# 26 of 88 gate and up pairs of a transformer kernel computed as a 2x2 block product of seven products

## The reference

```python
def swiglu(h, w_gate, w_up, w_down):
    return (jax.nn.silu(h @ w_gate) * (h @ w_up)) @ w_down

x = x + 0.5 * swiglu(rms_norm(x, norm_w[i, 0]), ffn_w_gate[i, 0], ffn_w_up[i, 0], ffn_w_down[i, 0])
```

## Time and profile before

| | us |
|---|---|
| median of 3 runs | 2694.77 |
| lowest and highest | 2693.09, 2696.92 |
| the profiled execution, first to last instruction | 2692.5 |
| TensorE busy in it | 2635.1 (98%) |
| VectorE, ScalarE, GpSimd busy | 1632.1, 869.7, 653.6 |

### The profile page before, as it was taken

The page is one execution under the profiler, slowest core; times in us unless marked ns, Lnnn a source line. Parts: engine busy times, 40 slices in busy tenths (PEclk is TensorE's granted clock), DMA queues, the critical chain, the costliest instruction groups (busy, mean ns, idle before and its releaser), DMA issues.

```text
span 2692.5 us, 32765 instructions
## 1 busy us (share of the span) xinstructions
PE 2635.1 (98%) x12738; PEld 2184.7 (81%) x12738; DVE 1632.1 (61%) x2391; ACT 869.7 (32%) x1501; POOL 653.6 (24%) x700
## 2 busy tenths in 40 slices
PE   8999999999999999999999999999999999899998
PEld 6888887778778888888888889988888878777886
DVE  5344468988846545565455657754343477768996
ACT  3101125666611101121001135621001035537995
POOL 2111221222322211221211247722211141012220
PEclk9999999999999999999999999999999999999999
DMA  4333333333324434445445330023333364037995
GB/s 124 98 94 101 95 94 107 96 105 102 94 81 138 141 111 147 133 118 148 125 128 146 104 106 2 9 71 101 94 98 98 92 82 64 15 125 281 373 368 228
DMA packets 457067, 325.80 MB, mean 121 GB/s; under 512 B 34657, under 2 KB 421042, under 8 KB 456658
## 3 DMA queue, kind: packets, MB, share of 16 engines
q1 hardware_dynamic: 435240, 287.22, 36.3%
q10 hardware_dynamic: 15050, 28.08, 3.4%
q0 software_dynamic: 6624, 8.41, 0.9%
HBM read 323.06 MB, written 16.32 MB: 126 GB/s over the span
## 4 chain that ended last, share of the span: by engine, by line
PE 91%; DVE 5%; ACT 2%; DMA 1%; issue 1%; SPq 0%; POOL 0%; DVEq 0%; ACTq 0%; POOLq 0%
PE bank L254 24%; PE bank L256 24%; PE bank L255 24%; PE bank L1483 2%; PE bank L2953 2%; PE bank L2955 1%; PE bank L2954 1%; PE bank L1583 1%; PE bank L1777 1%; PE bank L1789 1%; PE bank L1551 1%; PE bank L2972 1%; PE bank L2974 1%; PE bank L2973 1%; PE bank L2936 1%
## 5 line engine op out<-in xcount | busy, mean ns | idle before, releaser
L254 PE MATMUL bank<-h_hi,w_hi 128*128 128x512 f32 x1992 | 789.6, 396 | 8.5 <-DVE w_lo L246 3.9
L256 PE MATMUL bank<-h_hi,w_lo 128*128 128x512 f32 x1992 | 776.4, 390 | 0.0
L255 PE MATMUL bank<-h_lo,w_hi 128*128 128x512 f32 x1992 | 775.9, 389 | 0.0
L232 POOL TENSOR_SCALAR w_hi<-w_lo_exact 128x1024 fp32r<-128x1024 f32 x325 | 361.9, 1113 | 1464.9 <-DMA w_lo_exact<-in_ffn_w_gate 390.5
L246 DVE TENSOR_TENSOR w_lo<-w_lo_exact,w_hi 128x1024 fp32r<-128x1024 f32 x369 | 455.1, 1234 | 145.1 <-POOL w_hi L232 133.4
L254 PEld LDWEIGHTS bank<-h_hi,w_hi 128*128 128x128 f32 x1992 | 374.2, 188 | 94.9 <-ACT h_hi L350 6.9
L255 PEld LDWEIGHTS bank<-h_lo,w_hi 128*128 128x128 f32 x1992 | 374.4, 188 | 79.3 <-issue 3.4
L256 PEld LDWEIGHTS bank<-h_hi,w_lo 128*128 128x128 f32 x1992 | 374.1, 188 | 78.7
L254 PE MATMUL bank<-g_hi,w_hi 128*128 128x512 f32 x704 | 273.9, 389 | 0.0
L255 PE MATMUL bank<-g_lo,w_hi 128*128 128x512 f32 x704 | 273.9, 389 | 0.0
L256 PE MATMUL bank<-g_hi,w_lo 128*128 128x512 f32 x704 | 273.9, 389 | 0.0
(11 more groups left out here) (490 smaller groups left out, 3830.5 us busy)
## 6 DMA issues: line engine op xcount, KB each, us to landing
w_lo_exact<-in_ffn_w_gate SPq DMA_DIRECT2D x88, 512.0 KB, 3.8
w_lo_exact<-in_ffn_w_up SPq DMA_DIRECT2D x88, 512.0 KB, 3.9
w_lo_exact<-in_ssm_w_in SPq DMA_DIRECT2D x48, 512.0 KB, 4.1
mod_w<-in_w_mod ACTq DMA_DIRECT2D x48, 512.0 KB, 3.8
e_lo_exact<-in_w_gate SPq DMA_DIRECT2D x46, 512.0 KB, 6.0
e_lo_exact<-in_w_up SPq DMA_DIRECT2D x46, 512.0 KB, 7.5
e_lo_exact<-in_w_down SPq DMA_DIRECT2D x46, 512.0 KB, 6.6
w_lo_exact<-in_ffn_w_down SPq DMA_DIRECT2D x32, 512.0 KB, 3.9
```

The lines of the kernel that those rows point to most:

```text
L232: ge.tensor_scalar(k.w_hi[:, u % SLOTS, :], k.raw[:, u % SLOTS, :], 1.0, 0.0, ALU.mult, ALU.add).then_inc(*k.up("w hi", u))
L254: te.matmul(k.bank[bank][:, :], hi, x_hi, start=first, stop=False)
L255: te.matmul(k.bank[bank][:, :], hi, x_lo, start=False, stop=False)
L256: return te.matmul(k.bank[bank][:, :], lo, x_hi, start=False, stop=stop)
```

## The change

Write the gate unit as four blocks of rows and columns: its upper half of rows (features 0 to 511) G1 and lower half G2, the same for the up unit, U1 and U2; and `h` as upper and lower half of the features and first and second half of the tokens. Gate and up of one pair are then a 2x2 block matrix times a 2x2 block matrix, which can be had from seven block products in place of eight, if sums of the blocks are formed first and the results are added up afterwards. A product is four 128 x 128 blocks by 256 tokens, three matmuls each, so a changed ("joined") pair has 84 matmuls of 256 columns where a plain one has 48 of 512.

The seven, in their order on TensorE: UP_1, DIFF, UP_2, SUM, GATE_2, SUM_LESS, SUM_LEAST (numbers 0 to 6). UP_1, UP_2 and GATE_2 use blocks of the weights as they are; DIFF, SUM, SUM_LESS and SUM_LEAST use sums that VectorE forms (`operand_sum_vector`). All seven are rounded by ScalarE (`operand_hi_scalar`, four blocks of 128, 512 columns) and their rest is taken by VectorE (`operand_lo_vector`); GpSimd does nothing for a joined pair. Four sums of the parts of `h` (`t_vector`) are formed once for a stage from an unrounded copy `h_exact`, which ScalarE makes at the start of the stage. Three products are copied out of PSUM by ScalarE and then added onto by the next product in the same half bank; VectorE adds up gate and up in `joined_sums_vector` and `joined_rest_vector`.

Joined are pairs 3, 5, 7, 9 of the first half and 0, 2, 4, 6, 8, 10 of the second in `ffn00` and `ffn11`, and 3, 5, 7 of the first half in `ffn01` and `ffn10`: 26 pairs. `w_hi` becomes a ring of eight half slots, in which a joined pair takes eight and a plain one four, and `split_pool` gets a wait for the half slots to be free (`hi_free`). For the pair after a joined one this is product 1 (DIFF) of the joined pair for its gate unit and product 3 (SUM) for its up unit. The side job's slots are moved: six to pairs 1, 4, 6, 8, 9, 10 and six to the down units.

Core of the diff:

```diff
-GATE_BANKS, UP_BANKS, DOWN_BANKS = (0, 1), (2, 3), (4, 5)
+GATE_BANKS, UP_BANKS, DOWN_BANKS = (0, 2), (1, 3), (4, 5)
+JOINED = {"ffn00": ((3, 5, 7, 9), (0, 2, 4, 6, 8, 10)), "ffn11": ((3, 5, 7, 9), (0, 2, 4, 6, 8, 10)), "ffn01": ((3, 5, 7), ()), "ffn10": ((3, 5, 7), ())}
...
+                if is_joined(stage, half, j):
+                    for i in range(N_PRODUCTS):
+                        k.entry_at[stage, half, j, i] = (e + i) % HI_SLOTS
+                        k.entry_free[stage, half, j, i] = free(e + i - HI_SLOTS)
+                        ends[e + i] = ("product", (stage, half, j, i))
+                    e += N_PRODUCTS + 1
+                    k.joined_units[gate] = [("operand lo", (stage, half, j, GATE_2)), ("operand sum", (stage, half, j, SUM))]
+                    k.joined_units[up] = [("operand lo", (stage, half, j, UP_2)), ("operand sum", (stage, half, j, SUM_LEAST))]
+                else:
+                    for u in (gate, up):
+                        k.hi_at[u] = e % HI_SLOTS // 2
+                        if half or j >= 2:
+                            k.hi_free[u] = free(e + 1 - HI_SLOTS)
+                        ends[e] = ends[e + 1] = ("unit", u)
+                        e += 2
...
 def split_pool(k, first, last):
...
+        if u in k.hi_free:
+            ge.wait_ge(*k.at(*k.hi_free[u]))
+        ge.tensor_scalar(k.w_hi[:, hi_slot(k, u), :], k.raw[:, u % SLOTS, :], 1.0, 0.0, ALU.mult, ALU.add).then_inc(*k.up("w hi", u))
...
+def joined_tensor(k, stage, half, j):
+    te = k.te
+    left, right = k.bank[GATE_BANKS[j % 2]], k.bank[UP_BANKS[j % 2]]
+    first, second = slice(0, HALF_T), slice(HALF_T, T)
+    t_part = lambda n: lambda q: (k.t_hi[n][:, q, :], k.t_lo[n][:, q, :])
+    h_part = lambda n, cols: lambda q: (k.h_hi[:, n + q, cols], k.h_lo[:, n + q, cols])
+    x_of = {UP_1: h_part(0, first), DIFF: t_part(BELOW), UP_2: h_part(KH, first), SUM: t_part(ACROSS), GATE_2: t_part(LAST),
+            SUM_LESS: t_part(SECOND), SUM_LEAST: h_part(KH, second)}
+    out_of = {UP_1: left[:, first], UP_2: left[:, first], SUM: left[:, second], SUM_LEAST: left[:, second],
+              DIFF: right[:, first], GATE_2: right[:, first], SUM_LESS: right[:, second]}
+    onto = {UP_2: UP_1, GATE_2: DIFF, SUM_LEAST: SUM}
+    for i in range(N_PRODUCTS):
+        te.wait_ge(*k.at("operand lo", (stage, half, j, i)))
+        if i in onto:
+            te.wait_ge(*k.at("copied", (stage, half, j, onto[i])))
+        if (half, j) == (0, JOINED[stage][0][0]) and i in (DIFF, SUM, GATE_2, SUM_LESS):
+            te.wait_ge(*k.at("t lo", (stage, {DIFF: BELOW, SUM: ACROSS, GATE_2: LAST, SUM_LESS: SECOND}[i])))
+        hi, lo = operand_hi(k, stage, half, j, i), k.s_lo[:, lo_slot(stage, half, j, i), :]
+        for q in range(KH):
+            x_hi, x_lo = x_of[i](q)
+            te.matmul(out_of[i], hi[:, span(q)], x_hi, start=i not in onto and q == 0, stop=False, skip_group_check=True)
+            te.matmul(out_of[i], hi[:, span(q)], x_lo, start=False, stop=False, skip_group_check=True)
+            ins = te.matmul(out_of[i], lo[:, span(q)], x_hi, start=False, stop=q == KH - 1, skip_group_check=True)
+        ins.then_inc(*k.up("product", (stage, half, j, i)))
...
 def ffn_scalar(k, stage, mod_tiles=None):
...
+            if (half, j) == (0, 0):
+                if stage == "ffn00":
+                    ae.wait_ge(*k.at("x", ("setup", KD - 1)))
+                for m in range(KD):
+                    ae.activation(k.h_exact[:, m, :], k.x[:, m, :], ACT.Copy, scale=gain(k, stage, m)).then_inc(*k.up("h exact", (stage, m)))
                 exp_tables(k)
                 inverse_rms_scalar(k, stage, D, 7)
                 ae.preload_act_table(ACT.Silu)
+            if then:
+                operand_hi_scalar(k, stage, half, j + 1, UP_1)
+            if j and is_joined(stage, half, j - 1):
+                silu_scalar(k, stage, half, j - 1)
+            if joined:
+                operand_hi_scalar(k, stage, half, j, SUM_LESS)
+            if j:
+                gate_hi_scalar(k, stage, half, j - 1, down)
             if (stage, half, j) == ("ffn00", 0, 4):
                 column_scalar(k)
-            ae.wait_ge(*k.at("scaled gate", (stage, half, j)))
-            ae.activation(k.act[:, :], k.act[:, :], ACT.Silu).then_inc(*k.up("act", (stage, half, j)))
+            if joined:
+                if half and j == JOINED[stage][1][0]:
+                    ae.wait_ge(*k.at("x", ((stage, 0), KD - 1)))
+                elif j != JOINED[stage][half][0]:
+                    ae.wait_ge(*k.at("joined", (stage, half, joined_before(stage, half, j), "gate second")))
+                copy_product_scalar(k, stage, half, j, UP_1)
+                copy_product_scalar(k, stage, half, j, DIFF)
+                operand_hi_scalar(k, stage, half, j, SUM_LEAST)
+                copy_product_scalar(k, stage, half, j, SUM)
+            if then:
+                for i in (SUM, DIFF, UP_2, GATE_2):
+                    operand_hi_scalar(k, stage, half, j + 1, i)
+            if not joined:
+                silu_scalar(k, stage, half, j)
+            if (half, j) == (0, 0):
+                for n in (BELOW, ACROSS, LAST, SECOND):
+                    t_hi_scalar(k, stage, n)
...
 def ffn_vector(k, stage, mod_tiles=None):
...
+            joined, then = is_joined(stage, half, j), j + 1 < HALF_FF and is_joined(stage, half, j + 1)
+            after = u0 + 2 * j + 2
+            if j and is_joined(stage, half, j - 1):
+                joined_rest_vector(k, stage, half, j - 1)
+            if then:
+                operand_sum_vector(k, stage, half, j + 1, SUM)
             if j:
                 gate_prod_vector(k, stage, half, j - 1, u0)
-            if (stage, half, j) != ("ffn00", 0, 0):
-                split_vector(k, u0 + 2 * j + 2)
+            if then:
+                operand_sum_vector(k, stage, half, j + 1, DIFF)
+                operand_lo_vector(k, stage, half, j + 1, UP_1)
+            if joined:
+                operand_lo_vector(k, stage, half, j, SUM)
+            if not then and (stage, half, j) != ("ffn00", 0, 0):
+                split_vector(k, after)
             if (stage, half, j) == ("ffn00", 0, 3):
                 column_vector(k)
             if j:
                 gate_lo_vector(k, stage, half, j - 1)
             elif half == 0:
+                t_vector(k, stage)
                 ve.wait_ge(*k.at("inverse rms", stage))
-            ve.wait_ge(*k.at("unit", u0 + 2 * j))
-            if half or j:
-                ve.wait_ge(*k.last("prod"))
-            ve.tensor_tensor(k.act[:, :], k.bank[GATE_BANKS[j % 2]][:, :], k.nr[:, :], ALU.mult).then_inc(*k.up("scaled gate", (stage, half, j)))
-            if (stage, half, j) != ("ffn00", 0, 0):
-                split_vector(k, u0 + 2 * j + 3)
-            if mod_tiles:
-                mod_add(k, mod_tiles[half], j, half)
+            if joined:
+                operand_sum_vector(k, stage, half, j, SUM_LEAST)
+                operand_lo_vector(k, stage, half, j, SUM_LESS)
+            if then:
+                operand_sum_vector(k, stage, half, j + 1, SUM_LESS)
+            if not joined:
+                ve.wait_ge(*k.at("unit", u0 + 2 * j))
+                if half or j:
+                    ve.wait_ge(*k.last("prod"))
+                ve.tensor_tensor(k.act, k.bank[GATE_BANKS[j % 2]][:, :], k.nr[:, :], ALU.mult).then_inc(*k.up("scaled gate", (stage, half, j)))
+            if then:
+                for i in (DIFF, UP_2, GATE_2):
+                    operand_lo_vector(k, stage, half, j + 1, i)
+            if joined:
+                operand_lo_vector(k, stage, half, j, SUM_LEAST)
+            if not then and (stage, half, j) != ("ffn00", 0, 0):
+                split_vector(k, after + 1)
+            if half == 0 and j in (1, 2):
+                for n in (BELOW, ACROSS, LAST) if j == 1 else (SECOND,):
+                    t_lo_vector(k, stage, n)
+            if mod_tiles and j in MOD_J:
+                mod_add(k, mod_tiles[half], MOD_J.index(j), half)
+            if joined:
+                two_less_vector(k, stage, half, j)
+                joined_sums_vector(k, stage, half, j)
```

More of the change, by code:

```diff
@@ L622, in ffn_units, with is_joined, joined_before, plan_joined @@
     return u, u + 2 * HALF_FF
+def is_joined(stage, half, j):
+    return j in JOINED[stage][half]
+def joined_before(stage, half, j):
+    return max([i for i in JOINED[stage][half] if i < j], default=None)
+def plan_joined(k):
+    k.hi_at, k.hi_free, k.joined_units, k.entry_at, k.entry_free = {}, {}, {}, {}, {}
+    for stage in ("ffn00", "ffn01", "ffn10", "ffn11"):
+        for half in range(2):
+            u0, down = ffn_units(k, stage, half)
+            ends = {}
+            e = 2 * u0
+            for u in range(u0 - SLOTS, u0):
+                ends[2 * u] = ends[2 * u + 1] = ("unit", u)
+            def free(entry):
+                while entry not in ends and entry > 2 * u0 - HI_SLOTS:
+                    entry -= 1
```

(51 more changed lines are left out.)

204 lines of the change are left out of this document (172 added, 32 removed).

## The result

| | median of the runs | runs | profiled span |
|---|---|---|---|
| before | 2695.85 us | 2693.09 to 2697.96 | 2692.5 us |
| changed | 2734.74 us | 2732.64 to 2737.07 | 2735.8 us |

A forecast was written before the change was run, and what follows sets the result against it. TensorE, busy 98% of the span, was taken as the bound. -23.4 saved + 28.8 + 1.0 (product 5) + 5.8 + 0.6 (stage starts) = +12.8 us, so 2707.6 us; range 2683 to 2723.

The forecast's parts named there:

- Saved on TensorE: Joined pairs: 84 matmuls of 256 columns at 0.1188 us replace 48 of 0.2267; 0.90 us a pair, 23.4 us in all.
- The late product 5: SUM_LESS waits for VectorE's rest: 1.2 us late in 24 joined pairs (28.8), 0.5 in two others (1.0).
- the aside: In a joined pair, SUM_LEAST may slip in before GpSimd's turn; the rest for SUM_LESS then ends at 8.03, not 8.14.
- the sign to look for: In the profile after, in joined pairs: SUM_LEAST on VectorE at 1.5 us instead of 0.7.
- The start of `ffn00`: Copies and sums ahead of the first scaling make TensorE 3.1 late, then DIFF 1.3 and SUM 0.8; 5.8 us together.
- The start of `ffn01`: Four sums after VectorE's clearing make `w_lo` of pair 1's up unit ready at 839.2, TensorE asking at 838.8: 0.6 us.
- The side job: Moved transfers and additions in plain pairs and down units cost nothing, since VectorE has room there.
- 1 us a slot of excess: Side job: the price of each slot if VectorE's room in plain pairs and down units is gone.
- The slots of `w_hi`: A joined pair's slots come free when its operands are formed, before its matmuls end, so no transfer starts later.
- GpSimd's turn: Joined pairs: GpSimd's rounding holds VectorE 0.92 us before SUM_LESS; rival that it costs nothing: 2687.4 us, chance 0.15.
- the waits ahead of every product: Rival: TensorE waits at all seven products of each joined pair, 0.08 us each, 14.6 us more, 2722; chance 0.18.
- VectorE falls behind: Rival: more turns lost to GpSimd cost 1 us more a joined pair, 26 us, 2734; chance 0.08.

The follow-up runs named there:

- Two experiments: Each against the changed kernel: `w_lo` put behind the rest for SUM_LESS, 2705.38 us; GpSimd rounding the following up unit only after product 5, 2716.11 us.

## Why the direction was right and the size wrong

**Saved on TensorE.** Forecast 23.4, measured 21.2: the pace of 256 columns is 0.1198 us, inside the bounds given, not 0.1188.

**The late product 5.** Forecast 28.8 + 1.0, measured 28.1. Chain, place and size are as written, the order is that of the aside: the sign to look for was SUM_LEAST at 1.5 us, but it took 0.68, and the rest behind it took 1.34. Two experiments took the delay away in the parts it was built from.

**The start of `ffn00`.** Forecast 5.8, measured 6.5 (6.3 at pair 2, 0.2 at the second product of pair 3) and 0.4 that stands in the 28.1, but by another sum. VectorE and TensorE, where the earlier trace rows had 38.90, 41.52 and 43.11:

```profile
43.35 0.68 DVE L1069 TENSOR_TENSOR norm_sq<-bank,norm_r 128x512 f32<-128x512 f32 x1
...
45.41 1.22 DVE L258 TENSOR_TENSOR w_lo<-w_lo_exact,w_hi 128x1024 fp32r<-128x1024 f32 x1
...
46.77 0.77 PE L266 MATMUL bank<-h_hi,w_hi 128*128 128x512 f32 x1 [3.19 <-DVE w_lo L258]
47.33 0.63 PE L267 MATMUL bank<-h_lo,w_hi 128*128 128x512 f32 x1
```

The scaling and `w_lo` came as forecast (42.9 and 44.9 there, everything 0.5 later here), and so did the wait. What followed was not DIFF and SUM of pair 3 late by 1.3 and 0.8, but 13 matmuls at half the clock, 2.8 us; and with TensorE later by that, the operands of pair 3 were in time but for 0.2 us. A right number from a wrong addend.

**The start of `ffn01`.** Forecast 0.6 at the up unit of pair 1, measured 0.4 there and 0.4 at the second product of pair 3.

**The side job: the step that failed.** The prediction said "the plain pairs leave VectorE 2 us of room (20 against 22.1 above) and the down units more: nothing". Measured: 27.4 us, which is the whole of the 26 us between the forecast and the result. With the side job spread and all else as in the change, the kernel took 2708.9 us, where the forecast was 2707.6: the direction was right for the reasons given. The room on VectorE was there; it was not the resource. There is one buffer `mod_w`, and each load waits on ScalarE for the additions of the one before. Loads and additions of the changed kernel, as a tile (time from issue to landing, min/median/max; then the waits for it):

```profile
DMA to landing us min/median/max: 3.6/4.4/5.3
```

```profile
  DMA mod_w<-in_w_mod: 47.3, 24
```

In the kernel before it was 15.5 us in 5 waits.

4.4 for the transfer and 1.5 for the additions are 5.9 us a slot, in a down unit of 24 x 0.2267 = 5.44. In a pair of 10.88 the same slot would leave 5 us free. In the second halves ScalarE issues the load behind the `h_hi` of the residual, which waits for the residual, which stands behind the additions: a ring. That is read from the order on the queues; no run takes it apart, and at 10.9 us a slot it did no harm. The prediction named this term, gave it a price for the case that it should not fit ("1 us a slot of excess") and then left that price out of the sum and of the range. The room that it did count was VectorE's alone.

**The slots of `w_hi`.** "The slots of a joined pair come free when its operands are formed ... so that none starts later" was read for the slots of the raw weights. For those of `w_hi` it does not hold behind an odd number of joined pairs. Worth 15 us by the medians and 16 by the trace, but only through the chain above.

**The rivals.** GpSimd's turn did cost what was forecast; the waits ahead of every product, at 0.18, did not appear; "VectorE falls behind" gave the nearest time, 2734, and for no right reason: over the steady pairs VectorE never fell behind. The number of a rival is no evidence for it.

## What to carry to other kernels

When work is moved into shorter time slots, price its longest serial chain (issue, landing, use, release of the buffer) against the slot, not the load of the engine that does the work; and look at what stands behind it in an in-order queue, for a wait there costs whatever that is. When a saving of 0.8 us a pair meets a new wait of 1.1 us a pair, look for one instruction whose place makes the wait: here `w_lo`, moved behind three others in VectorE's order, was worth 29 us, and together with the spread side job it turned the loss into a gain. And once a stage has a deadline at its head, prepare operands where there is a gap, not simply later.
